# A two-block layer kernel whose two token tiles pass its four stage boundaries one after the other, with six split weight slots instead of four

## The reference

```
for layer in (0, 1):
    h = rms_norm(x, mix_pre_g[layer])
    m = pool_conformer_mixer(h)  if layer == 0 else  short_conv_mixer(h)
    x = x + rms_norm(m, mix_post_g[layer])
    h = rms_norm(x, ffn_pre_g[layer])
    x = x + rms_norm((relu(h @ w1) ** 2) @ w2, ffn_post_g[layer])      # d_ff = 8192
x = x + hybrid_layer(x)       # attention (8 heads), spatial gating, two gated projections, w_out
```

## Time and profile before

| | |
|---|---|
| median of 3 runs | 2813.27 us (2812.69 to 2816.14) |
| the profiled execution | 2813.65 us; its span from first to last instruction 2811.9 us |
| TensorE (PE) busy | 2742.8 us of 2811.9, 12357 matmuls and transposes |
| VectorE (DVE), ScalarE (ACT), GpSimd (POOL) busy | 1618.2, 1330.3, 310.6 us |
| mean granted TensorE clock | 0.992 of full speed |
| HBM read | 511.47 MB, 183 GB/s over the span |

### The profile page before, as it was taken

The page is one execution under the profiler, slowest core; times in us unless marked ns, Lnnn a source line. Parts: engine busy times, 40 slices in busy tenths (PEclk is TensorE's granted clock), DMA queues, the critical chain, the costliest instruction groups (busy, mean ns, idle before and its releaser), DMA issues.

```text
span 2811.9 us, 30563 instructions
## 1 busy us (share of the span) xinstructions
PE 2742.8 (98%) x12357; PEld 2269.4 (81%) x12357; DVE 1618.2 (58%) x1673; ACT 1330.3 (47%) x1617; POOL 310.6 (11%) x328
## 2 busy tenths in 40 slices
PE   8898899999999989999999999999999999999999
PEld 7677788888888878888788888888887888888887
DVE  5998644555555565555654555555556557655554
ACT  5665544444444454444454444444445546544443
POOL 2973100000000010000100000000011001100000
PEclk9999999999999999999999999999999999999999
DMA  7444555555555545555465555555554654455554
GB/s 242 136 150 154 170 186 185 190 194 192 184 193 187 192 159 196 193 189 186 154 205 195 187 187 194 182 194 193 184 191 154 198 183 162 165 195 194 194 180 164
DMA packets 259183, 515.55 MB, mean 183 GB/s; under 512 B 8114, under 2 KB 10724, under 8 KB 258532
## 3 DMA queue, kind: packets, MB, share of 16 engines
q1 hardware_dynamic: 259044, 513.60, 54.8%
HBM read 511.47 MB, written 2.10 MB: 183 GB/s over the span
## 4 chain that ended last, share of the span: by engine, by line
PE 90%; DVE 6%; issue 2%; ACT 1%; POOL 1%; DMA 0%; POOLq 0%; SPq 0%; ACTq 0%; DVEq 0%
PE bank L593 29%; PE bank L594 29%; PE bank L595 29%; DVE conv_out L1377 3%; PE bank L640 2%; DVE w_lo L579 2%; POOL acc L1551 0%; DVE x_res L1214 0%; DMA w_raw<-in_ab_w_in 0%; DVE A_lo L1169 0%; POOL small L1545 0%; ACT w_hi L572 0%; ACT conv_in L1097 0%; PE bank L739 0%; PE bank L798 0%
## 5 line engine op out<-in xcount | busy, mean ns | idle before, releaser
L579 DVE TENSOR_TENSOR w_lo<-w_raw,w_hi 128x1024 fp32r<-128x1024 f32 x960 | 1217.2, 1275 | 1006.4 <-ACT w_hi L572 1000.5
L572 ACT ACTIVATE w_hi<-w_raw 128x1024 fp32r<-128x1024 f32 x960 | 1013.1, 1060 | 1068.1 <-PE bank L595 1065.0
L593 PE MATMUL bank<-w_hi,A_lo 128*128 128x512 f32 x2432 | 958.5, 394 | 17.0 <-DVE w_lo L579 16.0
L595 PE MATMUL bank<-w_hi,A_hi 128*128 128x512 f32 x2432 | 949.9, 391 | 0.0
L594 PE MATMUL bank<-w_lo,A_hi 128*128 128x512 f32 x2432 | 949.7, 391 | 0.0
L593 PE MATMUL bank<-w_hi,B_lo 128*128 128x512 f32 x1408 | 552.0, 392 | 14.1 <-DVE w_lo L579 5.9
L593 PEld LDWEIGHTS bank<-w_hi,A_lo 128*128 128x128 f32 x2432 | 458.5, 189 | 116.7 <-DVE w_lo L579 21.6
L595 PE MATMUL bank<-w_hi,B_hi 128*128 128x512 f32 x1408 | 549.3, 390 | 0.0
L594 PE MATMUL bank<-w_lo,B_hi 128*128 128x512 f32 x1408 | 549.2, 390 | 0.0
L595 PEld LDWEIGHTS bank<-w_hi,A_hi 128*128 128x128 f32 x2432 | 458.3, 188 | 96.7
L594 PEld LDWEIGHTS bank<-w_lo,A_hi 128*128 128x128 f32 x2432 | 458.7, 189 | 92.5
(11 more groups left out here) (139 smaller groups left out, 841.5 us busy)
## 6 DMA issues: line engine op xcount, KB each, us to landing
w_raw<-in_ffn_w SPq DMA_DIRECT2D x256, 1024.0 KB, 5.1
w_raw<-in_w_in SPq DMA_DIRECT2D x88, 1024.0 KB, 5.0
w_raw<-in_sc_w_in SPq DMA_DIRECT2D x48, 1024.0 KB, 5.1
w_raw<-in_ab_w_in SPq DMA_DIRECT2D x24, 1024.0 KB, 5.2
w_raw<-in_ab_w_out SPq DMA_DIRECT2D x16, 1024.0 KB, 5.0
w_raw<-in_sc_w_out SPq DMA_DIRECT2D x16, 1024.0 KB, 5.0
w_raw<-in_w_out SPq DMA_DIRECT2D x16, 1024.0 KB, 5.0
w_raw<-in_w_proj_a SPq DMA_DIRECT2D x8, 1024.0 KB, 5.0
```

Of the source, the lines that this page charges most:

```text
L572: e.activation(w_hi[:, s % SPLIT_SLOTS, :], raw, ACT.Copy).then_inc(hi_made, 1)
L579: e.tensor_tensor(w_lo[:, slot, :], raw, w_hi[:, slot, :].bitcast(F32), ALU.subtract).then_inc(lo_made, 1)
L593: e.matmul(ps, lo[:, kt, tok], wh, start=first, stop=False)
L595: ins = e.matmul(ps, hi[:, kt, tok], wh, start=False, stop=last)
```

## The change

1. `SPLIT_SLOTS` goes from 4 to 6 and with it `AHEAD` from 3 to 5; the four steps by token tile stay four (`HELD = 4`). `dynamic_dma_scratch_size=1024` is given to the builder.
2. The order of steps is a table `SEQ`. In stages 1 to 4 the first two chunks f and f+1 go in turns: steps 0 to 3 of f, 0 to 3 of f+1, 4 to 7 of f, 4 to 7 of f+1. Weight loads follow `SEQ`.
3. A new `boundary(p)` in TensorE's program writes out the crossing: tile 0 of the four last steps; tile 1 of them, with the four transposes of (group 0, tile 0) ahead of the fourth; then steps 0 to 3 of chunk f for tile 0 and again for tile 1, each with the transposes of one group and one tile ahead of the steps that read them. Groups 2 and 3 are transposed for both tiles behind steps 0 and 2 of chunk f+1, whose first four steps read groups 0 and 1 only.
4. ScalarE's and VectorE's `boundary` make the halves of one group and one tile at a time (`hi_tile`, `lo_tile`: four instructions of 128x128 each, one signal behind the fourth), between the finishing chains of the tiles and the splits of the first six steps.
5. GpSimd takes the roots of both tiles before the last gains. The updates of groups 2 and 3 come behind those of groups 0 and 1 of both tiles.
6. Work that stood one step behind the end of a chunk is placed by `since(...)`, the distance in `SEQ`. Statistics of the new x move from step 3 of chunk f to its step 4.
7. The last four steps of the kernel are still done by tile, and nothing else moves.

The three functions `boundary` below are those of TensorE, ScalarE and VectorE, in this order.

```diff
-SPLIT_SLOTS = 4
+SPLIT_SLOTS = 6
+HELD = 4
...
+SCRATCH = 1024
...
+        SEQ = []
+        for first, end in zip(STAGE[:-1], STAGE[1:]):
+            rest = first
+            if first > 0:
+                for half in range(2):
+                    SEQ += [(c, 4 * half + i) for c in (first, first + 1) for i in range(4)]
+                rest = first + 2
+            SEQ += [(c, i) for c in range(rest, end) for i in range(n_steps[c])]
...
+        def split_steps(e, stage, one, at):
...
+            first, end = S0[STAGE[stage]], S_END[STAGE[stage + 1] - 1]
+            for s in range(first, end - HELD):
+                upto = s + AHEAD
+                if stage > 0 and s < first + HELD:
+                    upto = min(upto, first + AHEAD)
+                split_to(e, one, at, min(upto, end + SPLIT_SLOTS - HELD - 1))
+                yield SEQ[s]
+            split_to(e, one, at, end + SPLIT_SLOTS - HELD - 1)
...
+        def wait_step(e, c, i, which):
+            ch, s = chunks[c], POS[c, i]
             e.wait_ge(lo_made, s + 1)
             if i % 2 == 0:
-                e.wait_ge(lo_cast.sem, lo_cast.of(*ch.halves(ch.group0 + i * STEP_K // GK), 1))
+                g = ch.group0 + i * STEP_K // GK
+                e.wait_ge(lo_cast.sem, max(lo_cast.of(*halves_key(c, g, tt)) for tt in which))
...
+            def turn_tile(p, g, tt):
+
+                e.wait_ge(x_made.sem, x_made.of(p - 1, g, tt))
+                b4 = aux_begin("pre", p, g, tt)
+                for k in range(GK):
+                    f = g * CH + k * P
+                    ins = e.transpose(b4[:, k * P:(k + 1) * P], x[:, tt, f:f + P], ident)
+                ins.then_inc(aux_filled("pre", p, g, tt), 1)
...
+            def boundary(p):
+
+                c, f = STAGE[p] - 1, STAGE[p]
+                held_steps(c, (0,))
+                for i in range(n_steps[c] - HELD, n_steps[c]):
+                    if i == n_steps[c] - 1:
+                        turn_tile(p, 0, 0)
+                    step_matmuls(e, c, i, (1,), step_done)
+                for tt in tiles:
+                    if tt == 1:
+                        turn_tile(p, 0, 1)
+                    for i in range(HELD):
+                        if i == 2:
+                            turn_tile(p, 1, tt)
+                        wait_step(e, f, i, (tt,))
+                        step_matmuls(e, f, i, (tt,), step_done if tt == 1 else None)
...
+            def boundary(p):
+                f = S0[STAGE[p]]
+                squares(p - 1, NG - 1, 0)
+                split_to(e, split_hi, at, f + 2)
+                hi_tile(p, 0, 0)
+                split_to(e, split_hi, at, f + 3)
+                squares(p - 1, NG - 1, 1)
+                hi_tile(p, 1, 0)
+                split_to(e, split_hi, at, f + 4)
+                hi_tile(p, 0, 1)
+                split_to(e, split_hi, at, f + 5)
+                hi_tile(p, 1, 1)
...
+            def boundary(p, alone=False):
+                f = S0[STAGE[p]]
+                finish(p - 1, NG - 1, 0, alone)
+                settle(p - 1, 0)
+                update(p - 1, 0, 0)
+                split_to(e, split_lo, at, f + 2)
+                lo_tile(p, 0, 0)
+                update(p - 1, 1, 0)
+                finish(p - 1, NG - 1, 1, alone)
+                split_to(e, split_lo, at, f + 3)
+                lo_tile(p, 1, 0)
+                settle(p - 1, 1)
+                update(p - 1, 0, 1)
+                lo_tile(p, 0, 1)
+                update(p - 1, 1, 1)
+                split_to(e, split_lo, at, f + 4)
+                lo_tile(p, 1, 1)
+                for g in (2, 3):
+                    for tt in tiles:
+                        update(p - 1, g, tt)
+                    split_to(e, split_lo, at, f + 5)
...
                 for tt in tiles:
                     root(1, "postroot", "post", p, tt)
+                for tt in tiles:
                     gain(p, NG - 1, tt)
```

More of the change, by code:

```diff
@@ L472, in build @@
         load_row = []
[L473 to L474 removed]
+        for n in range(LOADS):
+            c, i = SEQ[STEPS_PER_LOAD * n]
+            load_row.append((c, i // STEPS_PER_LOAD))
         def at_chunk(c):
@@ L544, in store, with since, split_to @@
             e.dma_start(out_dram[:, tt, n * CH:(n + 1) * CH], x[:, tt, n * CH:(n + 1) * CH]).then_inc(out_written, 16)
[L547 to L563, removed]
+        def since(c, i, before):
+            return POS[c, i] - S_END[before]
+        def split_to(e, one, at, s):
+            while at[0] <= min(s, STEPS - 1):
+                one(e, at[0])
+                at[0] += 1
+        def split_steps(e, stage, one, at):
[7 more added lines that the diff above has]
+            split_to(e, one, at, end + SPLIT_SLOTS - HELD - 1)
         def split_hi(e, s):
@@ L657, in pe_program @@
             turn_x(0, 0)
[L660 to L691, removed]
@@ L693, in pe_program @@
+            boundary(1)
             pe_mlp(e, turn_x, turn_z, 0)
-            turn_x(2, 0)
-            turn_x(2, 1)
-            for c in range(C_L1, C_M1):
+            boundary(2)
+            for c, i in matmul_steps(e, 2):
                 j, part = divmod(c - C_L1, 3)
[L700 to L708, removed]
@@ L1278, in dve_program @@
-            dve_mlp(e, at, lo_plain, finish_tile0, finish_last, boundary, early, 0)
+            for c, i in split_steps(e, 0, split_lo, at):
+                if c >= 10 and i == n_steps[c] - 1:
+                    finish_last(0, c - 10)
+                if c == 0 and i in (0, 2, 4):
+                    lo_x(0, 1 + i // 2)
+                if (c, i) == (0, 6):
+                    e.wait_ge(par_made.sem, par_made.of("rows", 3))
+                    statistics(0)
+                if (c, i) in ((5, 2), (6, 1)):
+                    j = c - 5
+                    for h in two:
+                        kt = 4 * j + 2 * h
+                        lo_scaled("B", kt, [par_col("pool_scale", kt + k) for k in two], "mix", j, h)
+                for tap in taps_at(c, i):
+                    if tap[2] < 2:
+                        dve_tap(e, *tap)
+                if (c, i) in ((8, 3), (9, 0)):
+                    dve_norm(e, mean, c - 8)
+                if c == 9 and i in (2, 3):
+                    dve_silu(e, i - 2)
```

815 lines of the change are left out of this document (407 added, 408 removed).

## The result

| | before | after |
|---|---|---|
| median, runs side by side | 2814.01 us (4 runs) | 2829.88 us (4 runs, 2828.28 to 2831.66) |
| ratio, 95% interval | | 1.0056 [1.0038, 1.0073] |
| the profiled execution: time, span | 2813.65, 2811.9 us | 2828.28, 2826.6 us |

The account below looks back on a forecast made before the run. TensorE, busy 98% of the span, was taken as the bound. 2813.65 us - 3.2 (boundaries) + 14.4 (clock) + 0 gave 2824.9, at the median 2824.4 us; own range 2816 to 2829, wide range 2804 to 2831.

Parts of the forecast that it names:

- Waits at the boundary: At each boundary TensorE waits for the casts four times, 1.28 and three times 2.64 us, brackets about 1.1 and near 2.5.
- -3.2 us at full clock: Over four boundaries, the excess without clock loss goes from 42.4 to 39.2 us.
- The clock, +14.4: Three lowered clock stretches at each of four boundaries, 1.2 us each; +14.4 us in all, bounds 0 and 20.
- Six slots in the first stage, 0: First stage beside the taps: taken as 0, bounds -3 and +4 us, since VectorE's list of work is the same.
- start and lead, 0: ScalarE's splits and SyncE's loads have five steps of lead, 13.6 us, so their cost was put at 0.
- L686 at 227 +/- 3: Sign in the first stage: the transposes of the sum come at 227 +/- 3; before 222 the forecast is wrong.
- VectorE and ScalarE behind the crossing, 0: Behind each boundary, their finishing chains, updates and splits come in time for TensorE: cost 0, under a microsecond to spare.
- The rival that has VectorE late: `w_lo` of the new stage's sixth or seventh step comes late, 1.5 us more per boundary: 2830 us, chance 0.12.
- the clock holds: Rival: no lowered clock stretch at the boundaries, all else as forecast: 2810 us, chance 0.25.
- the slots pay: Rival: half of 14 us beside the first stage's taps comes back, clock holding at most boundaries: 2803 us, chance 0.15.

Follow-up runs that it names:

- experiment 1: The kernel before with six split slots and nothing else of the change: 2811.79 us, ratio 0.9984.
- experiment 2: The changed kernel with splits three steps ahead instead of five in the first eight steps of the first stage: 2830.13 us, ratio 1.0042.
- experiment 7: The changed kernel with a lead of three steps in place of five in the first stage: 2826.71 us, ratio 1.0037.
- experiment 6: The kernel before with six split slots, but splits only three steps ahead in the first stage: 2804.62 us, ratio 0.9960.
- experiment 4: The changed kernel with transposes issued one or more half-steps ahead of their readers, ScalarE's and VectorE's lists reordered to suit: 2795.35 us, ratio 0.9924.

## Why the prediction was right, and where it was not

The sign was right and the size near: +11.2 us forecast, +14.7 in the spans, +15.9 in the medians side by side. The median, 2829.88, lies inside the wide range near its upper end and 0.9 us above the forecast's own range of 2816 to 2829. Part of that nearness is luck: the clock's term was 3.3 too large, and the first stage's 5.8 had been put at 0. Step by step:

- **Waits at the boundary: right.** Brackets of "about 1.1 and three near 2.5" came as 1.06, 2.49, 2.44, 2.49. The parts of the sum came almost exactly: ScalarE 0.64 after the transposes (0.63 taken), four casts 1.14 (1.18), VectorE 1.12 (1.12), 3.09 in all (3.03). The nearest small forms of the trace priced a form that the kernel had never run.
- **-3.2 us at full clock: right in sum, mis-split.** Filled against unfilled before it is -2.2 (272.8 for 275.0). But it is made of -8.3 from the six slots (experiment 1) and +6.1 from the tile-wise order. The text counted for the slots only the late `w_lo`, and missed the split that stands ahead of `acc` and goes with it, which lengthens the wait for `x_res` by 1.14 at every boundary. Without the new order this change would have been a small gain (ratio 0.9984).
- **The clock, +14.4: the right mechanism, +11.1 measured.** Both factors were off, in opposite directions: twelve lowered stretches at 1.2 us were forecast, seven at 1.6 came. The number of seven belongs to the one execution traced: at the first boundary two other traces with the same waits have three (experiments 2 and 7), at the other boundaries all three traces have two each. The 1.2 had taken off a part "in which PE waits anyway"; nothing was to be taken off, because PE idles before the slow stretch and not in it. The Trainium skill (TensorE: Matmul & The Clock Gate, section "HAM oscillation — how this bites in real kernels") would have only longer idle gaps than these avoided; by it this term is 0. The granted clock of 0.57 behind waits of 2.44 to 2.49, and the 11.1 us that filling them brought back, speak against it here.
- **Six slots in the first stage, 0, and start and lead, 0: wrong.** +5.8 us, above the upper bound of +4. The text argued that VectorE's list of work is the same. The list is, but not the time that it takes: the loss that the text named as possible, GpSimd running ahead and its contention with VectorE moving, came (2.0 us more busy time for the same taps), and it stayed lost because slots that are all full tie ScalarE, and with it VectorE, to a PE that waits on VectorE (together 1.8). The larger part was missed: a longer lead moves splits ahead of other work on an engine's single list, and their weights have not arrived at 20 us (3.9). The sign that the text gave for this part, L686 at 227 +/- 3, failed: it came at 232.92. Experiments 6 and 7 give back 4.7 and 4.9 with the lead alone; the start's lead alone (experiment 2) gives back 0.6, with 1.6 lost to a lowered stretch.
- **VectorE and ScalarE behind the crossing, 0: right.** The rival that has VectorE late names 2830, the time that came, but its mechanism did not: the steps of the new chunks behind the held ones come 2.72 to 2.85 us apart, or 3.5 with eight transposes among them, and no `w_lo` wait stands there.
- The rivals "the clock holds" and "the slots pay" fell: the first by the stretches at 0.57, the second since VectorE's 156.9 us did not shrink (156.94 from its first tap at 71.39 to 232.80) and its idle time grew. Its number for the slots was not far off, though for another place.

What stays open: why a wait of this length is followed by a lowered stretch in one place and not in another, how the number of such stretches differs from execution to execution, and whether the last 3 us per boundary can be covered too; none of these was tried.

## What to carry to other kernels

Splitting a hand-over into pieces pays only if the engine that waits has other work between issuing a piece and reading it: against the old crossing with the same six slots, the four tile-wise crossings cost 17 us (11 of them the clock) with transposes directly ahead of their readers, and won 15 with them one or two half-steps earlier and the casters' lists set to match. Count a TensorE wait of about 2.5 us as up to 4, for the clock behind it, unless the low clock lies under another engine's work. And a deeper buffer is also a longer lead: where engines work through one list each, give the depth where it is needed and keep the lead short in stages whose bound is another engine.

## What the runs showed that was not expected

- TensorE idle for 2.44 to 2.49 us was followed by half clock in seven of twelve places, each 1.5 to 1.6 us long in loss. With the same waits 0.5 to 4 us elsewhere in time (experiments 2 and 7) it was three of three at the first boundary, for one.
- Behind a wait of 2.9 us the clock stayed at 1.00 and fell behind the next one, of 1.9 (experiments 2 and 4); the same program had it lowered behind a wait of 3.35 in another execution. The two differ by 1.6 to 1.8 us of time.
- 128x512 matmuls of no use in these waits cost nothing and saved 11.1 us; the same in a wait of 6.17 us, where the casts hid the low clock, saved 2.1.
- A split that stood one place too early on VectorE's list (1.21 us) lengthened PE's wait at each boundary by 1.14.
